# Half of the second-matrix pairs of a squared-ReLU MLP computed by seven block products, with the residual summed in DRAM

## The chip, the cores and the metric

The kernel runs on one core of one Trainium2 chip. The metric is device time in microseconds of one execution; each time is the median of several runs. PE is TensorE, DVE is VectorE, ACT is ScalarE, POOL is GpSimd, SP is SyncE.

## The reference

Two layers over 528 tokens (16 learned ones and 512 of the input) of width 1024. Each layer is a mixer (mLSTM in layer 0, differential attention in layer 1) and a squared-ReLU MLP, each behind an RMSNorm and added to the residual `h`. Only the MLP is touched here:

```python
def sq_relu_mlp(y, w_up, w_down):
    u = y @ w_up                                   # 1024 -> 4096
    return jnp.square(jax.nn.relu(u)) @ w_down     # 4096 -> 1024
...
    h = h + y
    h = h + sq_relu_mlp(rmsnorm(h, norm_gains[i, 1]), mlp_w_up[i], mlp_w_down[i])
```

## The kernel before

**Precision.** Every fp32 matrix is split into a high and a low half in fp32r: ACT copies the high half (`hi`), DVE subtracts it from the source (`lo`). A product is then three matmuls per 128-row slice: high by high, high by low and low by high.

**Pairs.** The MLP of a layer is 32 pairs. A pair is 256 columns of a weight matrix, loaded as one 1 MB tile `raw` by SP. The 4096 hidden units are taken in four groups of 1024. Each group is eight pairs: four "up" pairs (i % 8 = 0 to 3) that make 8 blocks of 128 hidden units, and four "down" pairs (i % 8 = 4 to 7) that use them for the 8 output blocks of `h`. I call the pairs of a group 0 to 7 and those of the next group 8 to 15; "pair 3" and "pair 11" stand in the same place of two groups. Layer 0 treats 528 tokens as two halves of 264, layer 1 treats 512 as two halves of 256 (one matmul of 512 columns in a plain pair).

**Plain pairs.** Each of the two 128-column halves m of the weights is multiplied by the whole input: 8 slices x 3 matmuls. All down pairs are plain. DVE adds each result from PSUM to `h` in SBUF (`evacuate`, L1571).

**Crossed pairs.** The up pairs from i = 2 on are multiplied as 2x2 blocks in the Winograd form, with seven products A11, A12, S2, S3, S1, S4, A22 where plain takes eight. DVE forms four sums of weight blocks per pair (`form`, L1493: S1, S3, S2, S4), ACT and DVE make their halves (`form_hi`, `form_lo` L1500 in two groups S23 and S14, `natural_lo` L1507 for A11 with A12 and for A22), and DVE combines the products from PSUM by seven additions (`total`, L1546: C11, U2, U3, C22, U4, C12, C21; ACT copies A11 to `t1` first). The sums of the input's blocks are made once per layer (`tl`, L1591).

**After an up pair** DVE applies the ReLU and the norm factor (L1551, L1567), ACT squares the result twice (fp32 into `abuf`, L946, high half into `ah`, L947), and DVE makes `al` (`act_lo`, L1557).

**Order.** Each engine's program is written out by hand: for each i the loop places the work for pairs i-1, i, i+1 and i+2 in a fixed order, and each engine works strictly in that order. DVE forms the weight sums of pair i+2 while PE works on pair i. Product n of a group uses PSUM bank n % 8, so a bank is taken again eight products later, and PE waits until DVE's addition has read it (`FREED` names which). SP loads pair i when the last low half of pair i-2 is made. POOL does nothing in the MLP, except that it builds masks for layer 1 in the last group of layer 0.

Of the kernel before, what the change touches and what calls it, by code (L numbers as in the profile page):

```python
# [80 lines left out]
def crossed(i):  # L81

    return is_up(i) and i >= PLAIN
# [18 lines left out]
RANK = counted(i for i in range(PAIRS) if crossed(i))  # L102
STEP = (counted(("gain_t", "meta_t0", "gate_mm", "u_t", "m_spread")) | counted(("hm_rd", "ym_hi", "ucol_rd"))
        | counted(("gain_rd", "ym_made", "gwh_done", "gw_ready", "ym_lo")))
N_DONE, N_READY, N_PLAIN, N_CROSSED = (len(x) for x in (DONE, READY, PLAINS, RANK))
# [3 lines left out]
FORM = {"S1": 0, "S2": 1, "S3": 2, "A22": 3}  # L109
UP_BANKS = [(0, 2, 4, 0), (4, 5, 4, 5)]  # L110


def bank_of(i, name):

    return (7 * (i % 8) + PRODUCTS.index(name)) % 8
# [35 lines left out]
LAST_BANKS = [0, 1, 2, 3, 0, 1, 0, 1]  # L151
# [53 lines left out]
def program(nc, a, out):  # L205
    with ExitStack() as ctx:
# [16 lines left out]

        h = new("h", [P, CB, T])
        y_at = cursor[0]
# [115 lines left out]
        ps = ctx.enter_context(nc.psum_tensor("ps", [P, 8, 512], F32))  # L341
        gate_rows = nc.dram_tensor("gate_rows", [2 * HEADS, T], F32).ap()
# [24 lines left out]
        yt_done, t_made, th_done, tl_done, t1_done = sems("yt_done t_made th_done tl_done t1_done")  # L367

# [74 lines left out]

        def last_use(i, item):

            p = i - 2
            if crossed(p):
                return DONE[p, item]
            return DONE[p, 1 if item in ("S4", "A22") else 0]

        def last_plain_use(i, m):
            p = i - 2
            if crossed(p):
                return DONE[p, "A22" if m else "A12"]
            return DONE[p, m]

# [101 lines left out]
        def _(pool):  # L558
# [69 lines left out]

            pool.wait_ge(m_done, DONE[PAIRS - 5, "A22"])
# [26 lines left out]
            with pool.Fori(0, HEADS - 1) as i:  # L656
                pool.wait_ge(sq_hi1, i + 1)
                nc.gpsimd.tensor_tensor(sqh1[aft, :], abuf[fore, NMETA:T], sqh1[fore, :].bitcast(F32),
                                        ALU.subtract).then_inc(sq_lo1, 1)


        @block.scalar
        def _(act):
# [246 lines left out]
            def mlp(layer, spans):  # L910
# [11 lines left out]
                def natural_hi(i, both):  # L922

                    act.wait_ge(m_raw[i % 2], 16 * (PAIRS // 2 * layer + i // 2 + 1))
                    act.wait_ge(m_done, items + last_use(i, "A12" if both else "A22"))
                    if both:
                        copy(hi[1 - i % 2][:, 0:8, :], raw[:, i % 2, :, 0:P]).then_inc(m_hi, 1)
                    else:
                        copy(hi[1 - i % 2][:, 24:28, :], raw[:, i % 2, 4:8, P:2 * P]).then_inc(m_hi, 1)
# [7 lines left out]
                def squares(i, m):  # L937
# [3 lines left out]
                    if crossed(i):  # L941
                        act.wait_ge(m_relu, 2 * (ranks + RANK[i] - 1) + m + 1)
# [3 lines left out]
                    nc.scalar.activation(ab[m][:, t0:T], tb[m][:, t0:T], ACT.Square).then_inc(sqa_done, 1)  # L946
# [12 lines left out]

                def finish(i, m):  # L960

                    if is_up(i):
# [10 lines left out]
                for i in range(PAIRS):  # L973
                    if i == 0:
# [3 lines left out]
                        for n in range(4):  # L978
                            forms_hi(n)
                    if crossed(i + 1):  # L980
                        form_hi(i + 1, "S23")
                    if crossed(i):
                        snap(i)
                    if crossed(i + 1):
                        form_hi(i + 1, "S14")
                    if i > 0 and not in_tail(layer, i - 1):
# [3 lines left out]
                    elif 1 <= i < PAIRS - 1:  # L990
                        plain_hi(layer, i + 1, 1)
                    if not crossed(i) and not in_tail(layer, i):
# [11 lines left out]
                    if crossed(i):  # L1004
# [191 lines left out]
        def _(dve):  # L1196
# [280 lines left out]
            def mlp(layer, spans):  # L1477
# [3 lines left out]
                def form(i, name, after):  # L1481
# [3 lines left out]
                    a11, a12, a21, a22 = r[:, 0:4, 0:P], r[:, 4:8, 0:P], r[:, 0:4, P:2 * P], r[:, 4:8, P:2 * P]  # L1485
# [17 lines left out]
                def natural_lo(i, both):  # L1503

                    dve.wait_ge(m_hi, layer * N_READY + READY[i, "A1" if both else "A22"])
                    rows, src = (slice(0, 8), raw[:, i % 2, :, 0:P]) if both else (slice(24, 28), raw[:, i % 2, 4:8, P:2 * P])
# [6 lines left out]
                def total(i, name):  # L1513
# [3 lines left out]
                    first, second = slice(t0, mid), slice(mid, T)  # L1517
                    if name == "C11":
                        dve.wait_ge(m_done, items + DONE[i, "A12"])
                        dve.wait_ge(t1_done, ranks + RANK[i])  # L1520
                        wait(dve, ah_done, block_of(i, 0) - 1)
                        o, x, y = tb[0][:, first], t1[:, 0:w], p("A12")
# [8 lines left out]
                    elif name == "C22":  # L1531
                        dve.wait_ge(m_done, items + DONE[i, "S1"])
                        dve.wait_ge(c_done, base + SUMS["U3"])
                        wait(dve, ah_done, block_of(i, 1) - 1)
                        o, x, y = tb[1][:, second], u3[:, 0:w], p("S1")
                    elif name == "U4":
                        o, x, y = u4[:, 0:w], u2[:, 0:w], p("S1")
                    elif name == "C12":
                        dve.wait_ge(m_done, items + DONE[i, "S4"])
                        dve.wait_ge(c_done, base + SUMS["U4"])  # L1540
                        o, x, y = tb[0][:, second], u4[:, 0:w], p("S4")
                    else:
# [10 lines left out]
                def act_lo(i, m):  # L1553
# [3 lines left out]
                    V.tensor_tensor(al[:, k, t0:T], ab[m][:, t0:T], ah[:, k, t0:T].bitcast(F32), ALU.subtract).then_inc(a_ready, 1)  # L1557

                def evacuate(i, m):
# [10 lines left out]
                    k = 2 * (i % 8) + m - 8  # L1570
                    V.tensor_tensor(tokens(h[:, k, :], spans), src, tokens(h[:, k, :], spans), ALU.add).then_inc(m_evac, 1)  # L1571
# [21 lines left out]
                for i in range(PAIRS):  # L1593
# [8 lines left out]
                    elif i > 0 and not is_up(i - 1) and not in_tail(layer, i - 1):  # L1602
                        evacuate(i - 1, 1)
                    if crossed(i + 1):
                        form_lo(i + 1, "S23")
                    if crossed(i - 1):
# [6 lines left out]
                    if crossed(i):  # L1613
                        total(i, "U2")
                    if is_up(i - 1):
# [14 lines left out]
                    elif not is_up(i) and not in_tail(layer, i):  # L1630
                        evacuate(i, 0)
                    after = crossed(i + 2)
# [16 lines left out]
                    if crossed(i):  # L1649
# [213 lines left out]
        def _(pe):  # L1863
# [228 lines left out]
            def mlp(layer, spans):  # L2092
# [24 lines left out]
                def plain_waits(i, m):  # L2117
# [6 lines left out]
                    if c >= 2:  # L2124
                        pe.wait_ge(m_evac, plains + c - 1)
                    if crossed(i - 1) and m == 0:
                        pe.wait_ge(c_done, 7 * ranks + summed(i - 1, "U3" if layer == 1 and i == PAIRS - 4 else "U2"))
                    if layer == 1 and i in (PAIRS - 4, PAIRS - 3):

                        pe.wait_ge(c_done, 7 * ranks + summed(PAIRS - 5, (("U3", "U4"), ("C12", "C21"))[i - PAIRS + 4][m]))  # L2130

                def product(i, name):

                    n = 7 * (i % 8) + PRODUCTS.index(name)
                    bank = n % 8
# [9 lines left out]
                    if n >= 8 and i - i % 8 + (n - 8) // 7 >= PLAIN:  # L2145

                        last, product_ = i - i % 8 + (n - 8) // 7, PRODUCTS[(n - 8) % 7]
# [4 lines left out]
                    elif 4 <= n < 8:  # L2152

                        u = 2 * (i - i % 8) - (2 if layer == 0 else 4) + ((n - 4) // 2 if layer == 0 else n - 4)
                        pe.wait_ge(m_evac, plains + PLAINS[u // 2, u % 2])
                    elif n == 0:
                        pe.wait_ge(c_done, 7 * (ranks + RANK[i] - 1))
                    row = 4 * SLOT[name]
                    for kb in range(4):
                        if name in FORM:  # L2160
                            mh, ml = th[:, FORM[name], kb, 0:w], tl[:, FORM[name], kb, 0:w]
                        else:
                            k, n0 = (kb if name == "A11" else 4 + kb), (mid if name == "S4" else t0)
                            mh, ml = yh[:, k, n0:n0 + w], yl[:, k, n0:n0 + w]
                        for n, (x, y) in enumerate(((hi, mh), (hi, ml), (lo, mh))):
                            last = mm(ps[:, bank, 0:w], x[1 - i % 2][:, row + kb, :], y,  # L2166
# [279 lines left out]
```

## Time and profile before

| | us |
|---|---|
| median of 3 runs | 1200.23 (1200.06 to 1201.15) |
| the profiled execution | 1199.86 |
| its span (first to last instruction) | 1198.1 |
| PE busy | 1189.4 (99%) |
| DVE busy | 910.2 (76%) |
| ACT busy | 643.9 (54%) |

Times below are positions in the span. Instructions of one engine overlap at their ends, so the distance from start to start is less than one instruction's duration. The granted PE clock is full (0.999), that is 2.4 GHz, over the whole run.

### The profile page before, as it was taken

Reading aid. Unit: us, or ns where it says so; the run is one execution under the profiler, and the core shown is the slowest. Engines: PE = TensorE matmul, PEld = TensorE weight load, DVE = VectorE, ACT = ScalarE, POOL = GpSimd, SP = SyncE. Lnnn points to the kernel's source line nnn. Section 1 sums busy time; section 2 is a strip of 40 time slices with the busy share of each in tenths; the row PEclk is TensorE's granted clock in tenths of the full one; section 3 lists DMA queues with packets and bytes.
Section 4 is the critical chain, followed back from the end, with each engine's and each line's share of the span. In section 5 each row is a group of like instructions: output and inputs, shape, how many; then the busy total and the mean of one; then the engine's idle time right before and its main releaser. Section 6 shows DMA issues by size and latency. Waiting matters only on the chain.

```text
span 1198.1 us, 22134 instructions
## 1 busy us (share of the span) xinstructions
PE 1189.4 (99%) x8665; PEld 1128.1 (94%) x8665; DVE 910.2 (76%) x1467; ACT 643.9 (54%) x1117; POOL 62.2 (5%) x105
## 2 busy tenths in 40 slices
PE   9999999999999999999999999999999999999998
PEld 8999999999999999999999999987798998988988
DVE  6899888888479488587568889887985875876863
ACT  6778877645244234234357887787542342433453
POOL 3211110000000000001010000000000000000000
PEclk9999999999999999999999999999999999999999
DMA  7343342323323323333232122213233333242322
GB/s 179 93 107 90 88 114 71 110 71 106 106 71 106 106 72 115 97 96 115 56 89 71 54 70 70 88 38 97 77 110 102 106 106 106 71 141 71 103 74 71
DMA packets 143122, 110.39 MB, mean 92 GB/s; under 512 B 22152, under 2 KB 142016, under 8 KB 143040
## 3 DMA queue, kind: packets, MB, share of 16 engines
q1 hardware_dynamic: 141600, 104.93, 29.1%
q0 software_dynamic: 1312, 4.22, 1.4%
q8 instruction: 57, 0.93, 0.3%
q14 instruction: 25, 0.20, 0.1%
q10 hardware_dynamic: 128, 0.09, 0.0%
HBM read 107.11 MB, written 2.13 MB: 91 GB/s over the span
## 4 chain that ended last, share of the span: by engine, by line
PE 81%; issue 16%; DVE 1%; ACT 1%; POOL 1%; DMA 0%; POOLq 0%; DVEq 0%
PE ps L2112 32%; PE ps L2166 24%; PE ps L1877 18%; PE ps L2384 2%; PE ps L1932 1%; PE ps L1950 1%; PE ps L2064 0%; PE ps L2029 0%; DVE wl L1202 0%; DMA meta_in<-in_meta_tokens_dram 0%; PE ps L2018 0%; ACT wh L665 0%; POOL khm L652 0%; PE ps L1893 0%; POOL qm L651 0%
## 5 line engine op out<-in xcount | busy, mean ns | idle before, releaser
L2112 PE MATMUL ps<-ah,hi 128*128 128x264 f32 (+1 forms) x736 | 192.6, 318 | 0.0
L2112 PE MATMUL ps<-al,hi 128*128 128x264 f32 (+1 forms) x736 | 192.5, 318 | 0.0
L2112 PE MATMUL ps<-ah,lo 128*128 128x264 f32 (+1 forms) x736 | 192.2, 318 | 0.0
L665 ACT ACTIVATE hi<-raw 128x1024 fp32r<-128x1024 f32 (+1 forms) x128 | 119.5, 957 | 133.6 <-PE ps L2112 133.6
L1877 PE MATMUL ps<-yh,wh 128*128 128x264 f32 (+1 forms) x704 | 160.5, 302 | 0.0
L1877 PE MATMUL ps<-yh,wl 128*128 128x264 f32 (+1 forms) x704 | 155.3, 295 | 0.0
L1877 PE MATMUL ps<-yl,wh 128*128 128x264 f32 (+1 forms) x704 | 155.3, 294 | 0.0
L2112 PEld LDWEIGHTS ps<-ah,hi 128*128 128x128 f32 x736 | 121.4, 188 | 9.9
L2112 PEld LDWEIGHTS ps<-al,hi 128*128 128x128 f32 x736 | 121.4, 188 | 9.8
L2112 PEld LDWEIGHTS ps<-ah,lo 128*128 128x128 f32 x736 | 121.3, 188 | 9.8
L2166 PE MATMUL ps<-th,hi 128*128 128x264 f32 (+1 forms) x448 | 126.6, 283 | 0.0
L2166 PE MATMUL ps<-tl,hi 128*128 128x264 f32 (+1 forms) x448 | 126.4, 282 | 0.0
L2166 PE MATMUL ps<-th,lo 128*128 128x264 f32 (+1 forms) x448 | 126.3, 282 | 0.0
L946 ACT ACTIVATE abuf<-tbuf 128x528 f32<-128x528 f32 (+1 forms) x64 | 40.8, 637 | 152.1 <-DVE tbuf L1551 148.5
L1571 DVE TENSOR_TENSOR h<-ps,h 128x528 f32<-128x528 f32 (+1 forms) x60 | 41.8, 697 | 97.6 <-PE ps L2112 97.6
L1877 PEld LDWEIGHTS ps<-yh,wh 128*128 128x128 f32 x704 | 112.0, 189 | 2.5 <-issue 0.4
L1877 PEld LDWEIGHTS ps<-yh,wl 128*128 128x128 f32 x704 | 111.1, 188 | 2.8
L1877 PEld LDWEIGHTS ps<-yl,wh 128*128 128x128 f32 x704 | 111.2, 188 | 1.6
L1447 DVE TENSOR_TENSOR lo<-raw,hi 128x1024 fp32r<-128x1024 f32 x72 | 87.8, 1222 | 17.8 <-ACT hi L665 16.8
L2166 PE MATMUL ps<-yh,lo 128*128 128x264 f32 (+1 forms) x336 | 94.9, 282 | 0.0
L2166 PE MATMUL ps<-yh,hi 128*128 128x264 f32 (+1 forms) x336 | 94.8, 282 | 0.0
L2166 PE MATMUL ps<-yl,hi 128*128 128x264 f32 (+1 forms) x336 | 94.7, 282 | 0.0
(300 smaller groups left out, 2723.1 us busy)
## 6 DMA issues: line engine op xcount, KB each, us to landing
raw<-in_mlp_w_up_dram SPq DMA_DIRECT2D x32, 1024.0 KB, 5.5
raw<-in_mlp_w_down_dram SPq DMA_DIRECT2D x32, 1024.0 KB, 5.1
raw<-in_diff_w_in_dram SPq DMA_DIRECT2D x24, 512.0 KB, 3.8
raw<-in_mlstm_w_in_dram SPq DMA_DIRECT2D x16, 512.0 KB, 5.1
raw<-in_mlstm_w_in_dram SPq DMA_DIRECT2D x16, 256.0 KB, 5.5
raw<-in_mlstm_w_out_dram SPq DMA_DIRECT2D x3, 1024.0 KB, 5.1
raw<-in_diff_w_out_dram SPq DMA_DIRECT2D x3, 1024.0 KB, 5.1
nmbc<-gate_rows POOLq DMA_DIRECT2D x8, 264.0 KB, 4.6
```

The costliest lines, as they stand in the source:

```text
L665: return nc.scalar.activation(o, i, ACT.Copy, scale=scale)
L946: nc.scalar.activation(ab[m][:, t0:T], tb[m][:, t0:T], ACT.Square).then_inc(sqa_done, 1)
L1447: V.tensor_tensor(lo[1 - i % 2][:, slots(i, m), :], raw[:, i % 2, :, P * m:P * m + P], hi[1 - i % 2][:, slots(i, m), :].bitcast(F32), ALU. ...
L1571: V.tensor_tensor(tokens(h[:, k, :], spans), src, tokens(h[:, k, :], spans), ALU.add).then_inc(m_evac, 1)
L1877: last = mm(ps[:, bank + s, 0:w_], w[:, slot, kb, :], m[:, kb, t0:t0 + w_], start=(kb == 0 and n == 0), stop=(kb == CB - 1 and n == 2))
L1932: last = mm(ps[:, b, c:c + t1 - t0], what(j), p, start=(b not in seen), stop=(n == 1 and i == len(passes) - 1))
L1950: last = mm(ps[0:rows, b, c:c + t1 - t0], ks[par][:, s0:s0 + rows], q[:, t0:t1], start=(m == 0), stop=(m == 1))
L2112: last = mm(ps[:, b + s, 0:cw], x[half][:, 20 * m + kb, :], y[:, kb, c0:c0 + cw], start=(kb == 0 and n == 0), stop=(kb == CB - 1 and n == 2))
L2166: last = mm(ps[:, bank, 0:w], x[1 - i % 2][:, row + kb, :], y, start=(kb == 0 and n == 0), stop=(kb == 3 and n == 2))
L2384: last = mm(ps[:, j % 2, 0:XH], x[half][:, 20 * m + kb, :], y[:, kb, c0:c0 + XH], start=(kb == 0 and n == 0), stop=(kb == CB - 1 and n == 2))
```

## The change

In the first three groups of each layer the down pairs 6 and 7 (`crossed_down`) are computed by the seven products as well. The down pairs 4 to 7 of these groups (`sent_down`) no longer add to `h` in SBUF. Instead POOL first copies `h` to DRAM (`h_sum`, 8 transfers), the results of a down pair go to `abuf` and `abuf1` (for the plain pairs 4 and 5 by ACT's `send`, for pairs 6 and 7 by DVE's additions), and POOL adds each to `h_sum` by an accumulating DMA of 128 x 528 fp32 (264 KB; 24 per layer). The next writer of the same buffer waits until the accumulation that reads it has landed (`h_sent`). After the third group one DMA brings `h` back.

The space of `h` holds meanwhile the squares of the group's 8 blocks in fp32 (`blocks_f`), of which DVE makes the four sums that the seven products need (`block_forms`, four additions of 1056 elements per partition, each waiting for the one before), ACT their high halves (`block_hi`) and DVE their low halves in place (`block_lo`). Two smaller edits: the waits of PE on PSUM banks at the borders of the groups are written bank by bank, and `LAST_BANKS` begins with 4, 5.

```diff
+def crossed_down(i):
+    return 0 <= i < PAIRS - 8 and i % 8 >= 6
+
+def sent_down(i):
+    return 0 <= i < PAIRS - 8 and i % 8 >= 4
...
-LAST_BANKS = [0, 1, 2, 3, 0, 1, 0, 1]
+LAST_BANKS = [4, 5, 2, 3, 0, 1, 0, 1]
...
+            def residuals(layer):
+                t0 = mlp_shape(layer)[0]
+                for k in range(CB):
+                    pool.wait_ge(h_ready, 16 * layer + k + 1)
+                    pool.dma_start(h_sum[k], h[:, k, :]).then_inc(h_saved, 16)
+                pool.wait_ge(h_saved, 16 * CB * (layer + 1))
+                for i in range(PAIRS):
+                    for m in range(2):
+                        if not sent_down(i):
+                            continue
+                        if crossed(i):
+                            pool.wait_ge(c_done, 7 * N_CROSSED * layer + summed(i, "C21" if m else "C12"))
+                        else:
+                            pool.wait_ge(m_evac, N_PLAIN * layer + PLAINS[i, m])
+                        pool.dma_start(h_sum[2 * (i % 8) - 8 + m, :, t0:T], ab[m][:, t0:T], accum_op=ALU.add).then_inc(h_sent[m], 16)
+                pool.wait_ge(m_done, N_DONE * layer + DONE[PAIRS - 9, "A22"])
+                for m in range(2):
+                    pool.wait_ge(h_sent[m], 16 * N_SENT * (layer + 1))
+                pool.dma_start(h[:, :, :], h_sum.rearrange("k p t -> p k t")).then_inc(h_back, 16)
...
+                def send(i, m):
+                    act.wait_ge(m_done, items + DONE[i, m])
+                    wait(act, h_sent[m], sent_before(layer, i))
+                    copy(tokens(ab[m][:, :], spans), plain_out(layer, i, m)).then_inc(m_evac, 1)
+
+                def block_hi(i, name):
+                    act.wait_ge(b_made, 4 * ((GROUPS - 1) * layer + i // 8 + 1))
+                    if name in ("S1", "A22"):
+                        act.wait_ge(m_done, items + DONE[i - i % 8 + 5, 1])
+                    copy(block_form(layer, name), blocks_f[:, :, BLOCK_FORM[name], 0:w]).then_inc(b_hi, 1)
...
+                    to = ab if crossed_down(i) else tb
+                    if name in ("C11", "C22"):
+                        m = int(name == "C22")
+                        if crossed_down(i):
+                            wait(dve, h_sent[m], sent_before(layer, i))
...
+                    if down and i % 8 == 6 and name in BLOCK_FORM:
+                        pe.wait_ge(b_lo, form_count(layer, i, name))
```

DVE, layer 0, first group, around pair 4, before (L1447 is a plain low half, L1571 the addition to `h`, L1507 and L1493 belong to the next crossed pair):

```order
L1551 SCALAR_TENSOR_TENSOR tbuf_118<-tbuf_118,rb 128x528 [waits c_done]
L1557 TENSOR_TENSOR al<-abuf,ah 128x528 [waits ah_done]
L1557 TENSOR_TENSOR al<-abuf_119,ah 128x528 [waits ah_done]
L1447 TENSOR_TENSOR lo_110<-raw,hi_109 128x1024 [waits m_hi]
L1571 TENSOR_TENSOR h<-ps,h 128x528 [waits m_done]
L1447 TENSOR_TENSOR lo_113<-raw,hi_112 128x1024 [waits m_hi]
L1571 TENSOR_TENSOR h<-ps,h 128x528 [waits m_done]
```

The same place after (L1618 is `natural_lo` and L1604 `form` of pair 6):

```order
L1557 TENSOR_TENSOR lo_112<-raw,hi_111 128x1024 [waits m_hi]
L1682 TENSOR_TENSOR blocks_f<-blocks_f 128x4x264 [waits a_ready,sqa_done]
L1684 TENSOR_TENSOR blocks_f<-blocks_f 128x4x264 [waits b_made]
L1686 TENSOR_TENSOR blocks_f<-blocks_f 128x4x264 [waits b_made]
L1688 TENSOR_TENSOR blocks_f<-blocks_f 128x4x264 [waits b_made]
L1618 TENSOR_TENSOR lo_115<-raw,hi_114 128x1024 [waits m_hi]
L1604 TENSOR_TENSOR lof_116<-raw 128x512 [waits m_done,m_raw0]
L1604 TENSOR_TENSOR lof_116<-raw 128x512 [waits m_done]
L1604 TENSOR_TENSOR lof_116<-lof_116,raw 128x512 [waits m_done,s_made]
L1604 TENSOR_TENSOR lof_116<-raw,lof_116 128x512 [waits m_done,s_made]
```

The additions to `h` are gone from DVE's queue; four block sums and the preparation of a crossed pair stand in their place.

DVE after, from pair 6's last additions to pair 7's first (L1662 is `total`; `abuf` is what the accumulation reads):

```order
L1662 TENSOR_TENSOR abuf<-u_119,ps 128x264 [waits c_done,m_done]
L1604 TENSOR_TENSOR lof_116<-lof_116,raw 128x512 [waits m_done,s_made]
L1604 TENSOR_TENSOR lof_116<-raw,lof_116 128x512 [waits m_done,s_made]
L1662 TENSOR_TENSOR abuf_121<-u_118,ps 128x264 [waits c_done,m_done]
L1611 TENSOR_TENSOR lo_115<-lof_116,hi_114 128x1024 [waits m_hi,s_made]
L1662 TENSOR_TENSOR abuf<-t_122,ps 128x264 [waits t1_done,m_done,h_sent0]
L1611 TENSOR_TENSOR lo_115<-lof_116,hi_114 128x1024 [waits m_hi,s_made]
```

Between the addition that completes `abuf` (C12 of pair 6) and the one that overwrites it (C11 of pair 7, behind `h_sent0`) stand four instructions of DVE, and POOL's accumulating DMA has to be issued and landed in that time.

## Rows read from the trace of the kernel before

**Rows 1.** The page: busy time by engine, and the chain that ended last.
```profile
PE 1189.4 (99%) x8665; PEld 1128.1 (94%) x8665; DVE 910.2 (76%) x1467; ACT 643.9 (54%) x1117; POOL 62.2 (5%) x105
...
PE 81%; issue 16%; DVE 1%; ACT 1%; POOL 1%; DMA 0%; POOLq 0%; DVEq 0%
```

**Rows 2.** The chain in order of time: start, us; down and up pairs, layers 0, 1.
```profile
382.78 46.74 PE ps L2112 x384
429.52 40.77 PE ps L2166 x336
...
974.34 44.63 PE ps L2112 x192
1018.96 39.69 PE ps L2166 x336
```

**Rows 3.** Windows: busy (count) of PE, PEld, DVE, ACT, POOL, then clock, DMA.
```profile
974.34:1018.96 44.62, 44.62 (x194) 36.07 (x194) 25.23 (x33) 13.23 (x15) 0.00 (x0) 1.00 0.38 118
1018.96:1058.66 39.70, 39.70 (x338) 39.70 (x337) 35.68 (x60) 19.06 (x29) 0.00 (x0) 1.00 0.25 81
```

**Rows 4.** DVE's timeline, layer 1, pairs 8 to 12: start, us, [idle before, releaser].
```profile
1021.84 0.42 DVE L1546 TENSOR_TENSOR tbuf<-t,ps 128x256 f32<-128x256 f32 x1 [0.35 <-PE ps L2166]
...
1024.69 0.42 DVE L1546 TENSOR_TENSOR u<-u,ps 128x256 f32<-128x256 f32 x1 [0.35 <-PE ps L2166]
...
1026.82 1.28 DVE L1493 TENSOR_TENSOR lof<-raw 128x512 f32<-128x512 f32 x2
...
1031.88 1.23 DVE L1500 TENSOR_TENSOR lo<-lof,hi 128x1024 fp32r<-128x1024 f32 x1 [1.30 <-ACT hi L665]
1033.02 0.69 DVE L1551 SCALAR_TENSOR_TENSOR tbuf<-tbuf,rb 128x512 f32<-128x512 f32 x1
...
1046.76 0.41 DVE L1546 TENSOR_TENSOR tbuf<-t,ps 128x256 f32<-128x256 f32 x1
...
1051.56 0.41 DVE L1546 TENSOR_TENSOR u<-u,ps 128x256 f32<-128x256 f32 x1
...
1063.59 0.69 DVE L1557 TENSOR_TENSOR al<-abuf,ah 128x512 fp32r<-128x512 f32 x1 [0.37 <-ACT ah L947]
1064.54 1.22 DVE L1447 TENSOR_TENSOR lo<-raw,hi 128x1024 fp32r<-128x1024 f32 x1 [0.26 <-ACT hi L665]
```

**Rows 5.** DVE's timeline, layer 0, the same places of the second group.
```profile
344.97 0.43 DVE L1546 TENSOR_TENSOR tbuf<-t,ps 128x264 f32<-128x264 f32 x1 [0.41 <-PE ps L2166]
...
347.89 0.43 DVE L1546 TENSOR_TENSOR u<-u,ps 128x264 f32<-128x264 f32 x1 [0.41 <-PE ps L2166]
...
387.29 0.71 DVE L1557 TENSOR_TENSOR al<-abuf,ah 128x528 fp32r<-128x528 f32 x1 [0.38 <-ACT ah L947]
```

**Rows 6.** DVE and ACT on the sums of the input's blocks, four instructions a row.
```profile
855.85 4.63 DVE L1591 TENSOR_TENSOR tl<-tf,th 128x1024 fp32r<-128x1024 f32 x4
...
259.87 4.76 DVE L1591 TENSOR_TENSOR tl<-tf,th 128x1056 fp32r<-128x1056 f32 x4
...
258.76 4.00 ACT L665 ACTIVATE th<-tf 128x1056 fp32r<-128x1056 f32 x4
```

**Rows 7.** DVE's last residual and ACT's first square of layer 1's MLP.
```profile
848.80 0.68 DVE L1437 TENSOR_TENSOR h<-ps,h 128x512 f32<-128x512 f32 x1
...
858.57 0.61 ACT L946 ACTIVATE abuf<-tbuf 128x512 f32<-128x512 f32 x1
```

**Rows 8.** DMA issues of the page, and one issue on POOL: KB each, us to landing.
```profile
nmbc<-gate_rows POOLq DMA_DIRECT2D x8, 264.0 KB, 4.6
...
60.58 0.55 POOL L595 DMA_DIRECT2D nmbc<-gate_rows  x1
```

**Rows 9.** Landing times of transfers `nmbc`, `mbc` (POOL, 264 KB), `fin` (SP, 256 KB).
```profile
DMA to landing us min/median/max: 4.0/4.6/5.6
...
DMA to landing us min/median/max: 5.8/5.9/6.9
...
DMA to landing us min/median/max: 2.5/2.6/2.8
```

More of the change, by code:

```diff
@@ L367, in program @@
         yt_done, t_made, th_done, tl_done, t1_done = sems("yt_done t_made th_done tl_done t1_done")
+        h_saved, h_back, b_made, b_hi, b_lo = sems("h_saved h_back b_made b_hi b_lo")
+        h_sent = [sem(f"h_sent{m}") for m in range(2)]
         gate_dve, gate_act = sems("gate_dve gate_act ")
@@ L1648, in mlp @@
                         form(i + 2, "S2", 1)
-                    if crossed(i):
+                    if crossed(i) and is_up(i):
                         relu(i, 0)
@@ L2123, in plain_waits @@
                         pe.wait_ge(evac, u_out + 5 + 2 * i + m)
-                    if c >= 2:
+                    if c >= 2 and (layer == 0 or is_up(i)):
                         pe.wait_ge(m_evac, plains + c - 1)
[L2126 to L2130, printed above, removed]
+                    if i % 8 == 4:
+                        if m == 0:
+                            pe.wait_ge(c_done, 7 * (ranks + RANK[i - 1] - 1))
+                        if m == 1 or layer == 0:
+                            pe.wait_ge(t1_done, ranks + RANK[i - 1])
+                        if m == 1 and layer == 0:
+                            pe.wait_ge(c_done, 7 * ranks + summed(i - 1, "U2"))
+                    elif i % 8 == 5 and layer == 1:
+                        sums = ("C12", "C21") if i == PAIRS - 3 else ("C11", "U2")
+                        pe.wait_ge(c_done, 7 * ranks + summed(i - 2, sums[m]))
                 def product(i, name):
-                    n = 7 * (i % 8) + PRODUCTS.index(name)
-                    bank = n % 8
+                    n, down = place_of(i, name), crossed_down(i)
+                    bank, begun = n % 8, i - i % 8 + (6 if down else 0)
                     if name in ("A11", "S2", "S1", "A22"):
@@ L2151, in product @@
                             pe.wait_ge(c_done, 7 * ranks + summed(last, FREED[product_]))
[L2152 to L2157, printed above, removed]
+                    elif down:
+                        if n == 0:
+                            pe.wait_ge(c_done, 7 * (ranks + RANK[i] - 1))
+                        elif n in (4, 6):
+                            pe.wait_ge(m_evac, plains + PLAINS[i - 1, n // 6])
+                    elif n < 7 and crossed(i - 1):
+                        pe.wait_ge(c_done, 7 * ranks + (summed(i - 1, FREED[PRODUCTS[n + 1]]) if n < 6 else summed(i - 2, "C21")))
```

142 lines of the change are left out of this document (115 added, 27 removed).

## The prediction, made before the changed kernel ran

> **What bounds the kernel now.** I read the engines' busy times first, then the chain of work that ended last, then windows of one group, then DVE's timeline. PE is busy 1189.4 of 1198.1 us, and the chain is PE's nearly throughout [rows 1]. In the MLP the chain in order of time shows pure PE stretches without a gap: four plain down pairs take 46.74 us in layer 0 and 44.63 in layer 1, four crossed up pairs 40.77 and 39.69 [rows 2]. So every matmul taken out there counts in full, as long as no one makes PE wait. The one who could is DVE: busy 35.7 of 39.7 us while up pairs run, 25.2 of 44.6 beside down pairs [rows 3]. The change takes work from PE and gives DVE more, and to judge it one must follow DVE's queue.
>
> **What it removes from PE.** A plain down pair costs 46.74 / 4 = 11.69 us in layer 0 and 44.63 / 4 = 11.16 in layer 1; a crossed one 10.19 and 9.92, a product 1.456 and 1.418 [rows 2]. That saves 1.4925 x 6 = 8.96 us in layer 0 and 1.235 x 6 = 7.41 in layer 1, together **16.4 us**, if PE stays fed.
>
> **What DVE's queue then looks like.** From start to start DVE needs 1.14 us for an instruction of 1024 elements per partition (4.63 for four), 1.17 for 1056 (4.76 for four) [rows 6], 0.60 for a weight sum (1.28 for two that overlap) and 0.34 for an addition from PSUM; one whose successor waits for its result costs its full length, 1.22 to 1.25, and about 0.05 more [rows 4, 6]. A round is one group, from C11 of pair 8 to C11 of pair 16.
> First half of the round, C11 of pair 8 to the end of `al` of pair 11: 1063.59 + 0.69 - 1021.84 = 42.4 us in layer 1, 387.29 + 0.71 - 344.97 = 43.0 in layer 0. In it DVE waits for PE only once (0.35 and 0.41) [rows 4, 5]; its other waits are for ACT, which itself waited for DVE (1.30 behind the square of what DVE's ReLU made). This half doesn't get shorter when PE is ahead: 42.1 and 42.6 us.
> Second half, new: 12 low halves of 1024 (13.7), 3 of 512 (1.8), 16 weight sums (9.6), 14 additions (4.6 or 4.8), 4 low halves of blocks (4.6 or 4.7), 4 block sums in a chain (5.1 or 5.2), and some 2.0 of waits for ACT's high halves, which follow the last weight sum by one ACT copy of 1.0 [rows 6]: 41.3 us in layer 1, 41.7 in layer 0.
> So a round of DVE is 83.4 and 84.3 us, and one of PE 39.69 + 44.63 - 2.47 = 81.85 and 40.77 + 46.74 - 2.98 = 84.5. **DVE's dependent chain becomes as long as PE's round**, though it is busy only nine tenths of it.
>
> **The new wait, h_sent.** C11 of pair 7 overwrites `abuf`, which the accumulation of pair 6 reads; C12 of pair 6 completed it 2.87 us earlier (weight sums S2 and S4 1.2, C21 0.33, the high half by ACT and the low half S23 the rest). If L is the time from C12's end until DVE may pass, DVE loses D = L - 2.87. Behind it in DVE's queue stand all of pair 7's additions, on which PE's banks for pair 8 depend, and pair 9's low halves. No accumulating DMA is in the trace. The nearest rows are loads of the same size on the same queue: 4.0 to 5.6 us from issue to landing, median 4.6; those queued behind another 5.8 to 6.9; a 256 KB write to DRAM by SP's queue 2.5 to 2.8 [rows 8, 9]. With 0.2 for the two hand-overs the bounds of L are 2.8 and 7.1, and nothing excludes more, since an accumulation also reads DRAM and a 1 MB weight load overlaps it. I take the same queue and size: L = 4.8, **D = 1.9**. The same wait for the other half (C21 to C22) has about 2.3 us more room. The plain pairs' sends are 9 us or more apart, so their waits cost nothing up to that length.
> The Trainium skill (DMA: Bandwidth & Descriptors, "Anatomy of one DMA") fits a POOL transfer by 2.0 us plus bytes over 436 GB/s, 2.6 us for 264 KB. No load of this size on POOL's queue came under 4.0 here, so the rows speak against it; what it would give is the third rival.
>
> **Where PE gets caught.** I walked the queue from pair 4's first matmul (0) in layer 1. `al` of pair 3 ends at 5.6, the plain low half of pair 5 leaves DVE free at 7.0 [rows 4], the block sums end at 12.1, pair 6's low half and weight sums at 15.6, its three low groups (waiting for ACT until 16.2) at 19.1, two block lows 21.35, pair 7's low half and weight sums 24.9, its S23 low (ACT until 25.5) 26.6, block low S1 27.9, C11, S14, U2 29.6, block low A22 **30.8**. PE wants S1 at 22.31 + 4 x 1.418 = 27.98 and A22 at 30.8: nothing to spare. In layer 0 the same walk ends at 31.45 and PE wants A22 at 32.1; with 0.8 that is lost in waits for ACT a delay of up to 1.3 us is free there. This is gate one. Going on, C11 of pair 8 comes 4.8 + D after pair 8's start in layer 1 and 4.0 + D in layer 0, where today it comes after 2.9 and 3.0.
> Gate two is S4 of pair 11: it needs the bank that U4 of pair 10 frees, 1051.56 + 0.41 - 1021.84 - 0.35 = 29.8 us after C11 of pair 8 [rows 4], and PE is there 36.85 us after pair 8's start. C11 may be 7.0 us late (7.2 in layer 0).
> Now the rounds with D = 1.9. Layer 0: C11 at 5.9 after the first group; `al` of pair 11 is then 2.5 us later than in the walk, gate one costs 1.2; next C11 at 6.5, 3.1 later, gate one costs 1.75. Sum 2.9 us. Layer 1: the first group starts 0.5 earlier, C11 at 6.2, 3.0 later, gate one 3.1; then 6.6, 3.4 later, gate one 3.5. Sum 6.6 us. Gate two stays open in both. The last groups' plain down pairs absorb the rest, as their DVE is half idle [rows 3].
> **Sum:** 1199.9 - 16.4 + 2.9 + 6.6 = 1193.0 for the profiled execution; its difference of -6.9 from its own time, set against the median of 1200.2, gives **1193.4 us**.
>
> **Edits that cost nothing.** Saving `h`: the last residual ends at 849.5, and the first square that overwrites its space starts at 858.6 [rows 7], against a landing of at most 6.9 us. If that cover went, ACT would stand with pair 2's high halves behind it, for about as long. Bringing `h` back (2.2 MB): it starts some 10 us into the last group and is needed 31 us later, by the first down addition; twice the 5.1 to 5.5 us of a 1 MB load is well inside. ACT gains 4 sends and 4 block copies a group, about 7 us; it is half idle [rows 1], and its copies lie on the walk above. The waits by bank and `LAST_BANKS` save nothing, since PE doesn't wait today. No transfer is removed.
>
> **Rivals.**
> 1. *The accumulation is slow.* Speaks for it: read, add and write of DRAM, 128 rows, a weight load in the same time, and the 6.9 us of queued transfers. Above L = 5.2 gate two begins to cost as well, from L = 6.1 in every group, and a us of L then costs 5 to 6 us over both layers. The gain is gone at L = 6.2. At L = 7.1 gate one costs 2.5 twice in layer 0 and 3.8 twice in layer 1, and gate two 1.0 to 1.95 at each of the six up groups behind a changed one (9.5): 22.2 us against 16.4, so **1206 us**; at L = 8, 1211. This is the slower side.
> 2. *DVE isn't caught at gate one*, because I overrate the waits for ACT or DVE recovers between rounds; then only PE's saving counts, at most 1183.9 us, and with a third of the stalls 1187. For it: DVE is busy only 0.93 of a round by the counts above. Against: the 1.30 us waits are there in every formed pair today.
> 3. *The transfer lands in under 2.9 us*, by the skill's figure or by the write on SP's queue. Then D = 0, layer 0 has no stall, layer 1 1.2 + 1.6: 1186.6 us.
>
> **How the numbers follow.** The forecast (L from 4.2 to 5.7, 1191 to 1198) 0.47; rival 1 0.27, of which the part with L from 5.7 to 6.6 (0.10) ends within 0.2%, the rest slower; rival 2 0.16; rival 3 0.10. A measurement of this kernel can tell about 0.2% (2.4 us) from no change. Of the forecast 0.03 falls within that. Faster 0.70, same 0.13, slower 0.17. The range leaves out 0.1 on each side: 1185 to 1206.
>
> **What would show it.** In the profile after, PE should wait in the MLP for the first time: at S1 or A22 of pairs 14 and 22 for `blocks_r` (line L1695), little in layer 0 and 3 to 3.5 us each in layer 1, and hardly at all at pair 6. DVE should wait for `h_sent` at C11 of pair 7, 15 and 23 about 1.9 us each. Crossed down pairs should take 10.2 and 9.9 us where PE isn't stopped. Landings of `h_sum<-abuf` near 4.6 us bear out the term; 7 or more bear out rival 1, with PE waiting for `c_done` (L1662) at pairs 8 and 11. The prediction is wrong if PE waits at other places, such as pair 2 for the save of `h` or the last down group for its return, or if DVE's instructions slow down beside POOL's transfers.

## The result

| | median, us | range, us | runs |
|---|---|---|---|
| before | 1200.69 | 1200.06 to 1201.44 | 4 |
| after | 1193.63 | 1192.05 to 1194.94 | 4 |

The ratio is 0.994 with a 95% interval of 0.9923 to 0.9958. The profiled execution of after took 1193.44 us, span 1191.6, where that of before took 1199.86.

### The profile page after: what moved, and what is told of

Read it like the earlier page. It is cut to its first block, busy times and chain, and to the rows that moved or that the text cites. A ratio compares the mean times of both kernels' runs of the same rounds, so it can differ in the third digit from the quotient of the medians.

```text
span 1191.6 us, 22996 instructions
## 1 busy us (share of the span) xinstructions
PE 1176.0 (99%) x8809; PEld 1126.1 (95%) x8809; DVE 1013.5 (85%) x1623; ACT 696.8 (58%) x1201; POOL 113.7 (10%) x171
## 4 chain that ended last, share of the span: by engine, by line
PE 71%; issue 19%; DVE 5%; ACT 2%; DMA 1%; POOL 1%; SPq 0%; DVEq 0%; POOLq 0%; ACTq 0%
PE ps L2335 29%; PE ps L2027 18%; PE ps L2262 17%; PE ps L2553 2%; PE ps L2082 1%; PE ps L2100 1%; ACT hi L741 1%; DVE lo L1611 1%; DVE lof L1604 1%; DVE lo L1618 1%; DMA xin<-in_x_dram 1%; DVE tbuf L1662 1%; PE ps L2214 0%; DVE tbuf L1667 0%; DVE u L1662 0%
## 5 line engine op out<-in xcount | busy, mean ns | idle before, releaser
L741 ACT ACTIVATE hi<-lof 128x1024 fp32r<-128x1024 f32 x80 | 83.4, 1052 | 129.3 <-DVE lof L1604 122.7
L2335 PE MATMUL ps<-th,hi 128*128 128x264 f32 (+1 forms) x448 | 126.8, 283 | 0.1
L2335 PE MATMUL ps<-tl,hi 128*128 128x264 f32 (+1 forms) x448 | 126.4, 282 | 0.0
L2335 PE MATMUL ps<-th,lo 128*128 128x264 f32 (+1 forms) x448 | 126.3, 282 | 0.0
L1611 DVE TENSOR_TENSOR lo<-lof,hi 128x1024 fp32r<-128x1024 f32 x80 | 97.2, 1223 | 25.5 <-ACT hi L741 23.9
L2262 PE MATMUL ps<-ah,hi 128*128 128x264 f32 (+1 forms) x448 | 115.8, 316 | 0.1
L2262 PE MATMUL ps<-al,hi 128*128 128x264 f32 (+1 forms) x448 | 115.6, 316 | 0.0
L2262 PE MATMUL ps<-ah,lo 128*128 128x264 f32 (+1 forms) x448 | 115.3, 315 | 0.0
L2335 PE MATMUL ps<-yh,hi 128*128 128x264 f32 (+1 forms) x384 | 108.5, 283 | 0.1
L2335 PE MATMUL ps<-yh,lo 128*128 128x264 f32 (+1 forms) x384 | 108.4, 282 | 0.0
L2335 PE MATMUL ps<-yl,hi 128*128 128x264 f32 (+1 forms) x384 | 108.4, 282 | 0.0
L1028 ACT ACTIVATE blocks_f<-tbuf 128x528 f32<-128x528 f32 (+1 forms) x48 | 30.5, 636 | 105.3 <-DVE tbuf L1667 101.7
L697 POOL DMA_DIRECT2D h_sum<-abuf x48 | 40.8, 849 | 482.7 <-ACT abuf L741 350.5
L1312 DVE TENSOR_TENSOR wl<-raw,wh 128x1024 fp32r<-128x1024 f32 x64 | 78.4, 1227 | 7.8 <-ACT wh L741 6.5
L2335 PEld LDWEIGHTS ps<-th,hi 128*128 128x128 f32 x448 | 84.3, 188 | 0.4 <-issue 0.2
## 6 DMA issues: line engine op xcount, KB each, us to landing
h<-h_sum POOLq DMA_DIRECT2D x2, 2112.0 KB, 10.3
```

The lines of the kernel that those rows point to most:

```text
L697: pool.dma_start(h_sum[2 * (i % 8) - 8 + m, :, t0:T], ab[m][:, t0:T], accum_op=ALU.add).then_inc(h_sent[m], 16)
L741: return nc.scalar.activation(o, i, ACT.Copy, scale=scale)
L1028: nc.scalar.activation(square_out(layer, i, m), halves(tb[m][:, t0:T]), ACT.Square).then_inc(sqa_done, 1)
L1312: V.tensor_tensor(wl[:, k, :, :], raw[:, k // 2, :, P * (k % 2):P * (k % 2) + P], wh[:, k, :, :].bitcast(F32), ALU.subtract).then_inc(spli ...
L1611: V.tensor_tensor(lo[1 - i % 2][:, rows, :], lof[1 - i % 2][:, rows, :], hi[1 - i % 2][:, rows, :].bitcast(F32), ALU.subtract).then_inc(m_ ...
L2262: last = mm(ps[:, b + s, 0:cw], x[half][:, 20 * m + kb, :], y[:, kb, c0:c0 + cw], start=(kb == 0 and n == 0), stop=(kb == CB - 1 and n == 2))
```

## The profile after

The page: busy time by engine, then the chain that ended last (compare [rows 1]), then three kinds of DMA issues (KB each, median us to landing).

```profile
PE 1176.0 (99%) x8809; PEld 1126.1 (95%) x8809; DVE 1013.5 (85%) x1623; ACT 696.8 (58%) x1201; POOL 113.7 (10%) x171
...
PE 71%; issue 19%; DVE 5%; ACT 2%; DMA 1%; POOL 1%; SPq 0%; DVEq 0%; POOLq 0%; ACTq 0%
...
h_sum<-abuf POOLq DMA_DIRECT2D x24, 264.0 KB, 4.7
h_sum<-abuf POOLq DMA_DIRECT2D x24, 256.0 KB, 4.9
h_sum<-h POOLq DMA_DIRECT2D x16, 264.0 KB, 2.4
h<-h_sum POOLq DMA_DIRECT2D x2, 2112.0 KB, 10.3
```

PE is still busy 99%, but its share of the chain fell from 81 to 71%, and DVE's rose from 1 to 5%: the chain now runs through DVE in places. What waited, from the view of waits (engine, line, releaser: us in total, times, longest):

```profile
PE ps L2335 <- issue: 5.9, 4, 3.1
...
DVE abuf L1662 <- DMA h_sum<-abuf: 6.5, 5, 1.5
...
DVE abuf L1662 <- PE ps L2335: 3.0, 1, 3.0
```

L2335 is a crossed product's matmul, L1662 an addition of `total`, and DVE's wait is the one of C11 of pair 7, 15 and 23 for `h_sent`, at five of its six places. The last row is C11 of pair 7 in layer 1, the sixth place; the view names PE, but this too was the transfer, as shown below under the wait for `h_sent`. PE's four waits are the stops of the crossed down pairs. The chain in order of time (start, us) shows where they are in layer 0 (compare [rows 2]):

```profile
295.41 23.37 PE ps L2262 x192
318.78 61.19 PE ps L2335 x504
...
403.34 5.82 PE ps L2335 x48
409.16 0.41 issue
409.57 55.67 PE ps L2335 x456
...
494.42 0.79 issue
495.21 55.68 PE ps L2335 x456
550.89 9.11 PE ps L2262 x75
```

Two plain pairs take 23.37 us, and two crossed down pairs with the four up pairs behind them 61.19, which is six times 10.2. The first group is free of stops. In the second and third PE stops after 48 matmuls, four products of 12: A11, A12, S2 and S3 of pair 14 and 22 are done and S1 is next. In layer 1 (below, only PE's own pieces; between them the chain is on DVE and ACT):

```profile
883.09 22.29 PE ps L2262 x96
...
997.43 36.95 PE ps L2335 x300
...
1082.37 54.20 PE ps L2335 x456
1136.57 16.73 PE ps L2262 x72
```

PE's own timeline at those two places (start, busy, instruction, idle before and its releaser), pairs 14 and 22 of layer 1:

```profile
997.43 0.55 PE L2335 MATMUL ps<-ah,hi 128*128 128x256 f32 x1 [3.14 <-issue]
...
1082.37 0.35 PE L2335 MATMUL ps<-ah,hi 128*128 128x256 f32 x1 [1.60 <-issue]
```

**What PE's stops cost.** A group without stops is 23.37 + 61.19 = 84.56 us in layer 0; in layer 1 it is 22.29 + 59.53 = 81.82 (the 59.53 is a row of the runs e3 and e5 below). From pair 4 of the first group to pair 4 of the last, layer 0 took 550.89 - 295.41 = 255.48, which is 1.8 over three such groups, and layer 1 took 1136.57 - 883.09 = 253.48, which is 8.0 over. In layer 1 pair 12 starts at 965.72 and pair 20 at 1052.64, so its three groups lost 0.8, 5.1 and 2.1. Before, the same stretches were three times 87.51 and three times 84.32 [rows 2], so the change saved 8.9 + 7.5 = 16.4 us of PE work and gave back 9.8. The difference, 6.6, is the result: the profiled times differ by 6.4. **Layer 1 gained nothing, layer 0 all of it.**

**What sets PE's loss in layer 1.** From one restart of PE to the next, 997.43 to 1082.37, are 84.94 us. DVE's own round, from C11 of pair 8 to C11 of pair 16, is 84.93:

```profile
933.06 0.41 DVE L1662 TENSOR_TENSOR tbuf<-t,ps 128x256 f32<-128x256 f32 x1
...
1017.99 0.41 DVE L1662 TENSOR_TENSOR tbuf<-t,ps 128x256 f32<-128x256 f32 x1
```

No row of DVE between these two waits for PE; it waits for ACT, and 1.34 us for the transfer. So DVE's round without the transfer is 83.6 us, PE's is 81.82, and PE loses the difference, with the wait 3.1 us, in each round after the first stop. In layer 0 both are 85.64 us (409.57 to 495.21, and C11 from 344.44 to 430.08).

## The experiments

My theory was the one of the prediction: the dependent chain of DVE (weight sums, block sums, low halves) is as long as PE's round, and the wait for the accumulation on top of it makes `blocks_r` late. The rivals were that the accumulation alone is the cause, and that each changed group loses the same.

### e0: the changed kernel once more

No edit.

> The changed kernel itself once more, beside the variants of it, so that they are compared on one chip. Both theories: 0.994 of the kernel before, 1193 to 1195 us, with PE stopped for some 3.3 us at product S1 of pair 14 in layer 1 and less at the other three places.

Measured: 1193.48 us (1192.16 to 1195.2), ratio 0.9947 (0.9933 to 0.996). The result holds. In the profiled execution, reckoned in the same way, PE lost 2.2 us in layer 0 and 6.5 in layer 1; the scatter of 3 us is treated in the last section.

### e1: the accumulation of pair 6 reads other buffers

Pair 6's additions go to `tbuf` and `tbuf1`, which are idle there, and their accumulations count on semaphores of their own. So C11 of pair 7 finds `abuf` free, and the first writer of `tbuf` comes a pair later.

```diff
-                        pool.dma_start(h_sum[2 * (i % 8) - 8 + m, :, t0:T], ab[m][:, t0:T], accum_op=ALU.add).then_inc(h_sent[m], 16)
+                        b, done = (tb, h_part) if i % 8 == 6 else (ab, h_sent)
+                        pool.dma_start(h_sum[2 * (i % 8) - 8 + m, :, t0:T], b[m][:, t0:T], accum_op=ALU.add).then_inc(done[m], 16)
...
-                    to = ab if crossed_down(i) else tb
+                    to = ab if crossed_down(i) and i % 8 == 7 else tb
```

> The sums of pair 6 (14, 22) go to tbuf and tbuf1, which are free there, and those of pair 7 to abuf as before, so that C11 of pair 7 no longer waits for an accumulation issued 4.3 us earlier. Nothing else is moved, and the accumulations stay. Theory (DVE's dependent chain is as long as PE's round, and the wait of 1.1 to 1.5 us for h_sent lengthens it once a group): the wait of DVE for the transfer goes from 6.5 us to 0, layer 0 loses its 1.8 us of stops, layer 1 keeps 3 to 4 of its 7.9: 1187 to 1188 us. Rival A (the stops come from the block sums alone and the wait on the transfer lies in idle time of DVE): 1193 to 1194, no difference. Rival B (the transfers themselves disturb DVE or PE): no difference either, since they are all still there.

Measured: 1187.0 us (1186.92 to 1188.61), ratio 0.9886 (0.9871 to 0.9902). DVE has no wait for a transfer any more. The chain of e1 in layer 0 has no stop, and in layer 1 each group but the first keeps a shorter one:

```profile
404.83 61.19 PE ps L2342 x504
...
489.39 61.19 PE ps L2342 x504
```

PE's wait in e1:

```profile
PE ps L2342 <- issue: 2.6, 2, 1.3
```

So 6.5 us of the 9.8 hung on the wait for the accumulation. The rest, two stops of 1.3 us at S1 of pair 14 and 22 of layer 1, is there without any transfer in the way: DVE's round in layer 1 is 83.5 us here (C11 of pair 8 at 929.54, of pair 16 at 1013.03), still 1.7 more than PE's.

### e2: block halves ahead of the next pair's

The order alone is changed: DVE makes `block_lo` S1 and A22 before pair 7's `form_lo` S23, and ACT makes the high half of A22 right after that of S1.

```diff
-                    if crossed(i + 1):
-                        form_lo(i + 1, "S23")
...
+                        block_lo(i, "A22")
+                    if crossed(i + 1):
+                        form_lo(i + 1, "S23")
```

> The low halves of the block sums S1 and A22 are made ahead of pair 7's low half S23 in DVE's order, and ACT makes the high half of A22 right behind that of S1. Same instructions. Theory: product S1 of pair 14 and 22 can start 1.6 us earlier against DVE's queue, so gate one gives way by 1.6 us; but DVE's round is shortened only by its 0.5 us wait for ACT, and the delay that PE no longer takes at gate one is carried to the next group. So layer 0's 1.8 us go, layer 1's 7.9 fall to about 5 (the half clock after the 3.1 us stop goes as well): 1189 to 1191 us. Rival A (the stop is of its own making, 3.3 us that vanish when its operand comes earlier): all stops at S1 go, 1187. Rival C (the order doesn't matter, another wait takes its place at once): 1193.5.

Measured: 1187.7 us (1187.56 to 1189.28), ratio 0.9892 (0.9877 to 0.9907), better than I expected. DVE waits for the transfers as long as in after (8.7 us at six places, where in after it was 6.5 at five and 3.0 at the sixth), yet PE stops less:

```profile
PE ps L2333 <- issue: 2.1, 2, 1.4
...
DVE abuf L1661 <- DMA h_sum<-abuf: 8.7, 6, 1.7
```

The wait stands, and 5.8 us of its price are gone, because the low half that PE waits for moved ahead of another, which had 0.47 us of waiting for ACT and 1.14 of its own. The wait hurts only through what is queued behind it. But DVE's round in layer 1, 84.4 us (C11 of pair 8 at 930.38, of pair 16 at 1014.79), is only 0.5 shorter than in after. A good part of the gain is thus a reserve that each layer has once: the stop at pair 14 fell from 3.1 us to 0.7, that at pair 22 only from 1.6 to 1.4.

### e3: both

> e1_apart and e2_order together. Theory: both lengthenings of DVE's chain are gone, what is left of its excess over PE's round in layer 1 (about 1 us a group) fits into the reserve of the two gates: 1184 to 1186 us, PE without a stop over 1 us in the MLP, near the 1184 us that the removed matmuls alone give. Rival A: 1187, as e2_order alone. If the two gains only overlap, it stands at the better of the two.

Measured: **1183.92 us** (1183.85 to 1184.05), ratio 0.9861 (0.9846 to 0.9876). The chain of e3 in layer 1:

```profile
903.47 59.53 PE ps L2340 x504
...
985.29 59.53 PE ps L2340 x504
...
1072.96 54.12 PE ps L2340 x456
```

Only in the third group is a trace of a stop left (0.2 us). It would grow with more groups, as DVE's round is 82.9 us here (C11 of pair 8 at 927.38, of pair 16 at 1010.30), still 1.1 over PE's. This is 16.6 us under the 1200.52 of before on the same chip, PE's whole saving, and it beats both kernels.

### e4: a slower accumulation

Ahead of each accumulation of pairs 6 and 7 POOL issues a second one, of the same buffer into a scratch tensor, so that the buffer comes free later. (Four more copies at the start of each MLP fill the scratch.)

```diff
+                            pool.dma_start(h_junk[2 * (i % 8) - 8 + m, :, t0:T], ab[m][:, t0:T], accum_op=ALU.add).then_inc(h_sent[m], 16)
                         pool.dma_start(h_sum[2 * (i % 8) - 8 + m, :, t0:T], ab[m][:, t0:T], accum_op=ALU.add).then_inc(h_sent[m], 16)
```

> Ahead of each accumulation of pairs 6 and 7 POOL issues a second one of the same size, from the same buffer into a scratch area of DRAM (which is filled at the start by four more copies), and the next writer of the buffer waits for both. It is work added, nothing of the result changes. Theory: DVE's wait at C11 of pair 7 grows by the second issue on POOL, 0.85 us, and some of its transfer, to 2.3 to 2.8 us. By the rounds of the prediction each us of that wait costs about 4 us over both layers as long as gate two is closed, and more above it: 1197 to 1200 us. Rival A (the wait for the transfer is idle time anyway): under 1195.

Measured: 1205.26 us (1204.32 to 1205.76), ratio 1.004 (1.0024 to 1.0055): slower than before, and above what I expected. C11 of pair 15 on DVE's timeline of layer 1, of e4 and then of after:

```profile
1018.80 0.42 DVE L1666 TENSOR_TENSOR abuf<-t,ps 128x256 f32<-128x256 f32 x1 [3.57 <-DMA h_sum<-abuf]
```

```profile
1008.89 0.42 DVE L1662 TENSOR_TENSOR abuf<-t,ps 128x256 f32<-128x256 f32 x1 [1.34 <-DMA h_sum<-abuf]
```

I had expected the second transfer to add 1 us or so, by POOL's issue; it added 2.2 to the wait. PE's stops grew with it (e4's waits of PE), and PE now waited for banks too, the second row (0.5 us each at pairs 11 and 27 of layer 1, at product S2, while at S4, the prediction's gate two, it started about 0.3 late), as the prediction's first rival has it in kind:

```profile
PE ps L2339 <- issue: 11.3, 4, 3.1
...
PE ps L2339 <- DVE tbuf L1666: 0.9, 2, 0.5
```

2.2 us more wait cost 11.8 us against e0. By rows of e4: layer 0's three groups took 557.38 - 296.73 = 260.65 us, layer 1's 1147.80 - 890.13 = 257.67, that is 19.2 over groups without stops, where e0 has 8.6; in the first down pair of each layer's last group PE waited for `al` and lost another 0.5 and 0.6; and 1.3 us come from the start of the program, before any of this (last section). DVE waited 3.5 us on average at C11, in e0 1.4. The spans of the two profiled executions, 1203.4 and 1190.3, are 13.1 apart, as these parts make. So a us of wait cost (19.2 + 1.1 - 8.6) / 2.15 = 5.4 us, more than the 4 I had expected, and the wait was longer than expected; both together make the miss. Again PE's two restarts in layer 1 (1005.11 and 1092.28) are one round of DVE apart: 87.17 us, from 940.73 to 1027.90.

### e5: the block sums on one column

The four block sums add one column of each block instead of 264. What is left out is the rest of the sums; all else runs as in after.

```diff
-                    b11, b12, b21, b22 = (blocks_f[:, :, n, 0:w] for n in range(4))
+                    b11, b12, b21, b22 = (blocks_f[:, :, n, 0:1] for n in range(4))
```

> The four block sums are made of one column per block only (so the result is not the reference's); instructions, waits and their order stay, but DVE's chain is about 4.4 us a group shorter. Theory: gate one never closes, DVE's round is below PE's in both layers even with the wait for the transfer, and PE doesn't stop: 1183.5 to 1185 us. Rival (the transfer alone is what stops PE): still at least 3 us of stops, 1188 to 1190.

Measured: 1184.24 us (1183.32 to 1185.01), ratio 0.9863 (0.9848 to 0.9878). DVE is busy 25.5 us less in all, 4.3 a group, the accumulations are as slow as in after, and DVE waits for them:

```profile
DVE abuf L1662 <- DMA h_sum<-abuf: 8.0, 6, 1.5
```

PE runs through in both layers (chain of e5 in layer 1):

```profile
986.75 59.53 PE ps L2335 x504
```

This refutes the rival that the transfer alone is the cause: with the same wait of up to 1.5 us and DVE's work 4.3 us a group shorter, nothing is lost. The chain itself is shorter by less, since right behind the sums DVE now waits for ACT's high half of pair 6 (16.0 us in all at six places, 0.8 in layer 1's second group, 5.1 at most), and from C11 of pair 8 to C11 of pair 16 it takes 81.6 us, no longer than PE's round. e1 and e5 each take away one of two delays in the same chain; e5 takes all stops away, e1 two thirds of the loss.

### e6 and e7: one group and two groups

`crossed_down` and `sent_down` hold for the first group alone (e6) or the first two (e7) of each layer; the other groups run as before.

```diff
-    return 0 <= i < PAIRS - 8 and i % 8 >= 6
+    return 0 <= i < 8 * SEVEN and i % 8 >= 6
```

> The change in the first group of each layer only, groups two to four as before it. Theory: the first group starts with DVE's reserve and stops PE nowhere, so its two pairs give their full 2.98 + 2.47 us: 1195.1 us (0.9955). Rival (a cost of the block sums or of the DRAM residual that each group pays alike, 3.3 us a group): 1198.2.

> The change in the first two groups of each layer. Theory: the second group gives 2.98 us less 0.6 in layer 0, but in layer 1 its stop of 3.3 us with what hangs on it (half clock, pair 11; some 5.5 us together) is more than its 2.47: about 1196, a little slower than with one group, and then the third group brings it to 1193.5. Rival (each group alike): 1195.9 as well, but then with 1198.2 for one group; the two runs have to be read together.

Measured: e6 1194.54 us (1194.14 to 1195.92), ratio 0.9953 (0.994 to 0.9967); e7 1194.19 (1193.68 to 1195.53), ratio 0.9953 (0.994 to 0.9967). So one group gains about 6 us, of 16.4 / 3 = 5.5 calculated, a second at most a few tenths and the third 0.7: within the scatter, nothing. e7 was to be a little slower than e6 and came out equal. The chain of e6 in layer 1 from the first group's pair 6 on, and of e7 behind the second group's stop:

```profile
909.57 59.57 PE ps L2339 x504
969.15 44.63 PE ps L2263 x192
```

```profile
997.00 55.61 PE ps L2339 x456
```

In e7 the second group stopped PE for 2.4 us in layer 1 where I had expected 3.3, and layer 1's two groups lost 4.2 us, not 5.5. What a changed group leaves behind on DVE costs nothing if an unchanged one follows, as DVE is half idle beside plain down pairs [rows 3]; the stop falls into the next changed group, into which DVE comes late. That speaks against an equal price for each group, and for a delay that is handed on from round to round.

## Why the prediction was right

**PE's saving.** 16.4 us was worked out, 16.4 is what the rows of after give, and e3 and e5 realise it in full (16.6 and 16.1 us under before on the same chips).

**DVE's chain as long as PE's round.** Right; it is the step on which all hung, and e5 bears it out. Without the wait for the transfer a round of DVE was forecast at 83.4 us in layer 1 and 84.3 in layer 0; measured are 83.6 and 84.5 (85.64 from 344.44 to 430.08, less 1.16 of wait). The terms of its second half add up to 0.1 more than the prediction has, which changes nothing. The walk of the second half stands row by row in DVE's timeline of after (layer 1, second group): the block sums take, as walked, 5 us (the first and the fourth are shown), and S1's low half is the one that PE waits for.

```profile
976.46 1.22 DVE L1682 TENSOR_TENSOR blocks_f<-blocks_f 128x1024 f32<-128x1024 f32 x1
...
980.23 1.23 DVE L1688 TENSOR_TENSOR blocks_f<-blocks_f 128x1024 f32<-128x1024 f32 x1
...
994.97 1.22 DVE L1611 TENSOR_TENSOR lo<-lof,hi 128x1024 fp32r<-128x1024 f32 x1 [0.47 <-ACT hi L741]
996.11 1.22 DVE L1695 TENSOR_TENSOR blocks_r<-blocks_f,ah 128x1024 fp32r<-128x1024 f32 x1
```

996.11 + 1.22 is 997.33, and PE resumes at 997.43. From the end of `al` of pair 11 (975.06) that is 22.3 us, as walked (27.9 - 5.6). The row ahead of it is pair 15's S23, which e2 moves behind.

**Which gate.** S1 or A22, said the prediction, with next to no room at either (27.9 against 27.98 and 30.8 against 30.8); every stop is at S1. It comes first, and once PE has stopped there it wants A22 by as much later.

**The wait for `h_sent`.** Mis-sized. Forecast were 1.9 us; at five of six places it was 1.14 to 1.45, since the accumulation was over 4.2 to 4.5 us after C12's end, not 4.8 (and DVE would have come 3.0 us after it, not 2.87). The row I took it from, a load of the same size on POOL's queue with 4.6 us to landing, is near the medians of the accumulations, 4.7 and 4.9, but these range from 3.8 to 7.2 us, and the one that DVE waits for at pair 15 landed in 4.0. At the sixth place, C11 of pair 7 in layer 1, it was the other way round. The view puts this wait down to PE:

```profile
923.97 0.42 DVE L1662 TENSOR_TENSOR abuf<-t,ps 128x256 f32<-128x256 f32 x1 [2.97 <-PE ps L2335]
```

But PE had begun pair 7's third product at 918.16, so the two that C11 adds were long done. POOL's row and the landing of this one transfer say what it was: 918.27 + 5.7 is 923.97.

```profile
918.27 0.84 POOL L697 DMA_DIRECT2D h_sum<-abuf  x1 [11.11 <-DVE abuf L1662]
...
DMA to landing us min/median/max: 5.7/5.7/5.7
```

So here the wait was 3.0 us, 6.0 after C12's end; in e0 it was 1.46 at the same place. Why this transfer took 5.7 us stays open.

**What PE's stops cost.** Forecast 2.9 us in layer 0 and 6.6 in layer 1; measured 1.8 and 8.0 in after, 2.2 and 6.5 in e0. Layer 0 is smaller as the wait is. In layer 1 PE resumes at pair 14 at 997.43, and without a loss it would have been at S1 at 883.09 + 81.82 + 27.98 = 992.89: 4.5 us lost where 3.1 was forecast. The slow transfer explains this, as in e0, without it, the same loss is 3.0: only in after do products of pair 11 start late (0.8 us together, the first sign of gate two) and pair 12's matmuls with `al` (0.5). The next round loses 84.94 - 81.82 = 3.1 us, forecast 3.5; the last 0.3 are matmuls that start late behind the restart. The half clock behind the first stop (last section) adds nothing to this sum: what PE lost by it made the next stop shorter, as DVE's round decides when PE resumes. The sum, 9.8 against 9.5, is closer than its terms, five waits shorter than forecast and one longer; that closeness is luck.

**The rivals.** The first, a slow accumulation, has the right mechanism and nearly the price. It named 5 to 6 us of time for each us of wait, the gain gone at a length of 6.2 us and 1206 at 7.1, which makes about 1203 at 6.6; e4 cost 5.4 for each and came to 1205.3 at 6.6 (in its second group C12 ends at 1012.20 and C11 starts at 1018.80), 1.3 of it by its start. The second, that DVE isn't caught at all, is refuted by after, but describes e3. The third put the landing under 2.9 us. In after, the plain copies of `h` to DRAM on the same queue land in 2.4 us; the accumulations take 4.7. By the fit of the Trainium skill (DMA: Bandwidth & Descriptors, "Anatomy of one DMA") an estimate for this size is 2.6 us. With the plain copy's 2.4 the trace agrees, with the accumulation's 4.7 it doesn't.

**The edits at no cost.** The save of `h` is waited for by no one on PE's path. The return lands in 10.3 us, about the "twice 5.1 to 5.5" that was set against 31, and nobody waits for it. The stretches ahead of the changed groups, between them and behind them are as long as before, within 0.15 us each.

## What to carry to other kernels

When work is moved from the engine that bounds to one that is 76% busy, walk the second engine's queue through one whole round, with each dependent result at its full length: a gain that repeats holds for the first round and is lost from the second on, as far as the second engine's round is the longer one. Before giving such a change up, look at what stands right ahead of the instruction that the first engine waits for. One exchange of order and one other pair of buffers brought 9.6 us here, more than the change itself had brought.

## What the runs showed of the hardware

**Behind some stops PE ran at half clock; what that costs depends on what comes next.** Windows of after and then of e4 (stretch: length, busy and count of PE, PEld, DVE, ACT, POOL, then granted clock, DMA share, GB/s), from the first matmul behind a stop in layer 1:

```profile
997.40:1000.20 2.80, 2.77 (x13) 2.80 (x14) 2.80 (x5) 1.10 (x2) 0.00 (x0) 0.50 0.01 1
1000.20:1003.00 2.80, 2.80 (x25) 2.80 (x25) 2.80 (x7) 0.00 (x0) 0.00 (x0) 0.99 0.34 58
```

```profile
1005.11:1007.91 2.80, 2.80 (x15) 2.80 (x16) 2.80 (x5) 1.06 (x2) 0.00 (x0) 0.58 0.01 1
...
1092.28:1095.08 2.80, 2.80 (x24) 2.80 (x24) 2.80 (x5) 1.06 (x2) 0.00 (x0) 1.00 0.00 0
```

After the stop of 3.14 us at pair 14 the granted clock was 0.50, that is 1.2 GHz, for 2.8 us, and 13 matmuls ran where 24 do at full clock: 11 x 0.118 = 1.3 us of PE's work late. In after this didn't lengthen the run: PE resumed at pair 22 one round of DVE later (84.94 us against 84.93), so the stop there was shorter instead, and the same holds in e4 (87.17 and 87.17). In e7, where an unchanged group follows, it stayed lost: from the restart at pair 14 to the next plain down pair PE took 55.6 us, without any delay it would be 59.53 - 5.67 = 53.9, and 0.3 of the difference is there behind stops at full clock too. In e4 it fell so after the stop of pair 14 (3.13 us) but not after that of pair 22, which was as long, nor after two of 2.5 us in layer 0. In e0 it fell to 0.60 after 2.85 us and in e7 to 0.68 after 2.41, both at pair 14 of layer 1; after 1.6 us and less it stayed full (1.00) in the stretches behind such stops in after, e0, e1 and e2. The Trainium skill (TensorE: Matmul & The Clock Gate, "Part 1") says that an idle array falls back to half rate and that activity lifts it again. Four of the seven stops of 2.4 us and more here agree; what sets the other three apart stays open.

**The start scatters by 1.3 to 1.7 us.** In e1, e2, e4 and e5 PE waits 2.1 to 2.6 us in total for the first load of the input, in after and e0 0.6 to 0.7, and in before, e3 and e7 not at all. This is the row of e1's waits; e1's piece of the chain at 404.83 begins in e3 at 403.22, 1.6 us earlier:

```profile
PE ps L2186 <- DMA xin<-in_x_dram: 2.6, 2, 2.1
```

The execution of e1 that this is read from took 1188.61 us, its others 1186.92 to 1187.07. So profiles are to be compared stretch by stretch, and only medians as whole times. The changed kernel scatters by more (e0 3.0 us, after 2.9), but long stops alone aren't the reason, as e4, with the longest, scatters by 1.4. Of the 1.3 us between the profiled executions of after and e0, 1.2 are PE's losses (9.8 against 8.6): 1.6 more in layer 1, where the one transfer was slow, and 0.4 less in layer 0. Whether landings spread the other executions too, no run here shows.

**An accumulating DMA.** POOL is held 0.85 us by the issue of one and 0.54 by that of a plain copy of the same size (rows of after: instruction, count, duration ns min/median/max, first and last start):

```profile
L697 POOL DMA_DIRECT2D h_sum<-abuf x48: 836/847/902, 306.8 to 1102.5; - x48
L687 POOL DMA_DIRECT2D h_sum<-h x16: 539/540/595, 221.0 to 842.9; - x16
```

It lands in 4.7 to 4.9 us by the median, between 3.8 and 7.2, where the plain write takes 2.4. With a second one issued right behind it the buffer came free 2.2 us later still (e4, pair 15: 6.3 us from the first issue against 4.1 in after), more than the 0.85 that an issue takes.
